# Gate chain, decays, key and value rows and output gating moved under the input projection; linear-attention outputs with tokens on partitions

## The chip, the cores and the metric

The kernel runs on one core of one Trainium2 chip. Its time is the time on the device of one execution, in microseconds; the median of three runs is shown. A profile was taken of one further execution.

## What is computed

One inference step of a one-layer hybrid decoder: 1024 prompt tokens and 8 new tokens (each with 4096 past tokens), width 1024, all in fp32. Cut to what matters here:

```python
h = rms_norm(x, norm_mix_pre)
z = h @ w_in       # gq 256, gk 256, gv 512, gr 512, glr 16, nq 512, nkv 768, ng 24 columns
g = log_sigmoid(glr @ w_gla_gate + b_gla_gate) / 16
# gated linear attention, 4 heads, chunks of 64 tokens:
b  = cumsum(g, within the chunk)
qe = gq * 64 ** -0.5 * exp(b)
a  = tril(qe @ (gk * exp(-b)).T)
o  = a @ gv + qe @ S
S  = exp(b_last) * S + (gk * exp(b_last - b)).T @ gv
y_gla = rms_norm(o, per head) * gain * silu(gr)
# native sparse attention, 8 query heads, 2 key heads: compressed keys and values
# (a convolution of 32 rows with stride 16, + pe, gelu, @ w2), selected blocks, a window,
# mixed by sigmoid(ng); with 1024 tokens the prompt selects every block
x += rms_norm(concat(y_gla, y_nsa) @ w_out)
x += rms_norm(relu(rms_norm(x) @ w_ff_up) ** 2 @ w_ff_down)
```

The new tokens take one step of the recurrence each, with their own state, and attend to their paged cache. Outputs are also the new key and value rows, the window rows and the states.

## The kernel before

Phases follow each other, each a block with one instruction stream per engine; a phase starts when all engines have left the one before: load, norm, input projection, middle phase, prompt attention, sample attention, output projection, norm, feed-forward, norm. Activations lie features on partitions: `hT` is the normed input (8 tiles of 128 features by 1032 tokens), `Z` holds the projected tiles (24 of them).

**Dense phases.** Input projection, output projection and feed-forward use Strassen's way of multiplying with seven products (helper `seven_products`, matmul at L291). A pair of output tiles is seven products M1, M2, M6, M5, M7, M3, M4 in that order, each of 16 matmuls (32 instructions for two, since an fp32 matmul is two instructions of which the profile counts each). The products accumulate in PSUM banks and are evicted by ScalarE (M1, M6, M5, M4: L526 in the projection) or added by VectorE (M2, M7, M3: L546). GpSimd makes four sums of weight blocks per pair (`weight_sums`, L254 to L261). The banks are given by `bank_of`: M1, M6, M7 and M4 use banks 0 and 1 or 2 and 3 by turns from pair to pair, M2 banks 4 and 5, M5 and M3 banks 6 and 7. M1 waits for the eviction of M4 two pairs back, M2 for that of M2 one pair back, M6 for M1, M7 for M6, M3 for M5, M4 for M7 of the same pair. The weights of a pair lie in one of two slots of `ring`; SP asks for pair n once M4 of pair n - 2 is done. The projection has 11 such pairs, the output projection 4, the feed-forward 32. In half of the feed-forward's pairs (down, all but the first group) VectorE evicts all seven.

**Small products.** After the 11 pairs the projection multiplies the 40 columns of the gates (16 of rank, 24 of the sigmoid gates) with all tokens (L517), in three parts of 344 tokens, and ScalarE evicts them.

**Middle phase** (`phase_mid`), in the order of TensorE: the gate products (L863, 16 rows deep); the transposes of key and value rows of each 128 tokens (`kv_rows`, L760 and L763, two row buffers in `srow`, evicted by ScalarE and VectorE by turns and stored by SP), with outer products for the new tokens' states between them (L771, from diagonals that GpSimd makes, L696); then the recurrence in eight steps of 128 tokens: scores (L796), state increments (L809), transposes of the next values and keys (L782, L784, evicted by ScalarE, L938 and L939), outputs (L821 within the chunk, L828 with the state); then the new tokens' outputs (L893, one column each), the bias products of the compression (L848, one column each), the compression's convolutions (L857) and the squares for the norm of the outputs (L839, ones times squares), and two last small products. Beside it ScalarE makes softplus, the exponentials of the decays, the sigmoids of `gr` and the root of the norm (as exponential of a logarithm, L1009 and L1014), VectorE the running sums (L1036), the decayed queries and keys (L1049 to L1053), mask (L1061), states (L1075) and at the end the gating (L1190, L1192). The outputs have features on partitions. ScalarE's queue asks for a 4 MB copy of the window rows from one DRAM tensor to another at the start (L957).

**Attention** (`phase_attend`) first scales the queries on VectorE (L1384) and its scores (L1415) wait for that.

What follows attention is touched by the change in one place only, the banks of the dense phases.

Of the kernel before, what the change touches and what calls it, by code (L numbers as in the profile page):

```python
# [80 lines left out]
def layout(nc, ctx, M):  # L81
# [29 lines left out]
    M.PS = ctx.enter_context(nc.psum_tensor("PS", [P, 8, 512], FP32))  # L111
    M.sems = {}
# [124 lines left out]
def bank_of(M, n, e):  # L237
    return {M1: 2 * (n % 2), M6: 2 * (n % 2), M7: 2 * (n % 2), M4: 2 * (n % 2), M2: 4, M5: 6, M3: 6}[e]
# [25 lines left out]
def seven_products(nc, M, pe, st, n, data, before):  # L264
# [37 lines left out]
def phase_norms(nc, M, A, O, use, front, back):  # L302
# [20 lines left out]
    with nc.Block() as block:  # L323
        @block.sync
        def _(sp):
            if use == 0:
                for s in range(2):
                    sp.dma_start(pair_slot(M, s), A["w_in"][0, :, 2 * s * P:2 * (s + 1) * P]
                                 .rearrange("(k p) c -> p k c", p=P)).then_inc(M.sem(f"pair{s}_loaded"), 16)
            elif back is not None:  # L330
# [130 lines left out]
def phase_project(nc, M, A):  # L461

    NP = 11
    w_in = A["w_in"][0].rearrange("(k p) c -> p k c", p=P)
    hsum, small_l, small = M.sem("proj_summed"), M.sem("small_loaded"), M.sem("small_done")
    Xf = M.X[:, :, :].rearrange("p a n -> p (a n)")
    h11, h12, h21, h22 = (M.hT[:, h * KQ:(h + 1) * KQ, t * HN:(t + 1) * HN] for h in range(2) for t in range(2))
    t1, t2, t3 = (Xf[:, i * KQ * HN:(i + 1) * KQ * HN].rearrange("p (k n) -> p k n", n=HN) for i in range(3))
    t4 = M.srow[:, 0:KQ * HN].rearrange("p (k n) -> p k n", n=HN)
    wsm = M.Zf[:, 23 * N:23 * N + KD * (RANK + NGATE)].rearrange("p (k c) -> p k c", k=KD)  # L470
    parts = [1] * 6 + [4] * 2 + [1] * 3
    st = M.dense = Seven(M, ["first"] * NP, parts, M.srow[:, 2064:3600], M.dense)

    def tiles(n):
        return M.Z[:, 2 * n, :], M.Z[:, 2 * n + 1, :]

    with nc.Block() as block_:
        @block_.sync
        def _(sp):
            for n in range(2, NP):  # L480
                st.wait_product(sp, n - 2, M4)
                w = pair_slot(M, n)
                if n < 6 or n >= 8:
                    c = 2 * n * P if n < 6 else C_KV + 2 * (n - 8) * P
# [87 lines left out]
def phase_mid(nc, M, A, O):  # L572
# [53 lines left out]
    def by(t):  # L626

        return rows[t % 2], t // 2 + 1
# [1586 lines left out]
```

## Time and profile before

| | |
|---|---|
| median of 3 runs | 2159.88 us (2159.83 to 2160.62) |
| the profiled execution's own time | 2160.74 us |
| its span in the profile | 2159.0 us |
| mean granted TensorE clock | 0.95 |
| TensorE busy | 1951.8 us, 90% of the span |
| ScalarE / VectorE / GpSimd busy | 492.3 / 699.1 / 618.0 us |

The profile gives, for each instruction, engine, line of the kernel, tiles and duration, and for idle time of an engine what ended it. PE is TensorE, PEld its weight loads, DVE VectorE, ACT ScalarE, POOL GpSimd, SP the engine that issues most transfers.
### The profile page before, as it was taken

Reading aid. Unit: us, or ns where it says so; the run is one execution under the profiler, and the core shown is the slowest. Engines: PE = TensorE matmul, PEld = TensorE weight load, DVE = VectorE, ACT = ScalarE, POOL = GpSimd, SP = SyncE. Lnnn points to the kernel's source line nnn. Section 1 sums busy time; section 2 is a strip of 40 time slices with the busy share of each in tenths; the row PEclk is TensorE's granted clock in tenths of the full one; section 3 lists DMA queues with packets and bytes.
Section 4 is the critical chain, followed back from the end, with each engine's and each line's share of the span. In section 5 each row is a group of like instructions: output and inputs, shape, how many; then the busy total and the mean of one; then the engine's idle time right before and its main releaser. Section 6 shows DMA issues by size and latency. Waiting matters only on the chain. (4 is left out here: it accounts for less than half of the span.)

```text
span 2159.0 us, 25959 instructions
## 1 busy us (share of the span) xinstructions
PE 1951.8 (90%) x10618; PEld 1554.0 (72%) x10618; DVE 699.1 (32%) x1541; ACT 492.3 (23%) x1089; POOL 618.0 (29%) x526
## 2 busy tenths in 40 slices
PE   3999995785899968999997996999999999999997
PEld 3888882572444436777775886888888888888885
DVE  2300002627565533423332107530132223213313
ACT  2001102334555543434332014101010000001002
POOL 0411212104888762111110304312221122111223
PEclk9999996787999988999998997999999999999998
DMA  4112104101000017665650411111111111111111
GB/s 119 38 45 39 40 20 147 41 23 40 1 1 1 1 34 262 226 200 189 224 178 30 133 36 25 38 40 39 40 40 59 39 40 39 46 52 39 40 50 79
DMA packets 121806, 149.62 MB, mean 69 GB/s; under 512 B 29888, under 2 KB 107496, under 8 KB 113432
## 3 DMA queue, kind: packets, MB, share of 16 engines
q1 hardware_dynamic: 109824, 76.64, 12.2%
q0 software_dynamic: 9216, 67.11, 9.3%
q10 hardware_dynamic: 2648, 4.21, 0.5%
q8 instruction: 84, 1.38, 0.3%
q14 instruction: 34, 0.28, 0.0%
HBM read 139.86 MB, written 12.27 MB: 70 GB/s over the span
## 5 line engine op out<-in xcount | busy, mean ns | idle before, releaser
L291 PE MATMUL PS<-Z,ring 128*128 128x258 f32 x1152 | 258.2, 380 | 0.0
L1581 PE MATMUL PS<-Z 128*128 128x256 f32 (+1 forms) x1024 | 244.6, 385 | 0.0
L291 PEld LDWEIGHTS PS<-Z,ring 128*128 128x128 f32 x1152 | 218.2, 189 | 32.9
L291 PE MATMUL PS<-hT,ring 128*128 128x258 f32 x992 | 224.9, 384 | 8.8 <-DMA ring<-in_w_out 7.7
L254 POOL TENSOR_TENSOR Z<-ring 128x512 f32<-128x512 f32 x36 | 48.7, 1353 | 602.1 <-PE PS L291 532.7
L291 PEld LDWEIGHTS PS<-hT,ring 128*128 128x128 f32 x992 | 190.0, 192 | 38.2 <-DMA ring<-in_w_out 7.7
L1581 PEld LDWEIGHTS PS<-Z 128*128 128x128 f32 x1024 | 186.5, 190 | 43.0 <-issue 20.5
L2127 ACT ACTIVATE Z<-PS 128x516 f32<-128x516 f32 x80 | 48.0, 600 | 646.8 <-PE PS L291 646.8
L291 PE MATMUL PS<-Z 128*128 128x258 f32 x832 | 187.1, 380 | 0.0
L291 PEld LDWEIGHTS PS<-Z 128*128 128x128 f32 x832 | 157.5, 189 | 23.9
L2147 DVE TENSOR_TENSOR Z<-PS,Z 128x516 f32<-128x516 f32 x96 | 66.8, 696 | 314.9 <-PE PS L291 314.9
L291 PE MATMUL PS<-hT,Z 128*128 128x258 f32 x640 | 145.9, 380 | 0.0
L1544 POOL DMA_INDIRECT Z<-in_cache_nsa_kv,idx x64 | 60.2, 941 | 275.1 <-ACT X L1766 101.9
L291 PEld LDWEIGHTS PS<-hT,Z 128*128 128x128 f32 x640 | 121.1, 189 | 18.4
L1285 POOL TENSOR_SCALAR Z<-Z,misc 128x63 f32<-128x63 f32 (+7 forms) x87 | 99.4, 1161 | 85.2 <-DVE misc L1370 85.0
L1872 DVE STREAM_TRANSPOSE Z<-Z 128x1024 f32<-128x1024 f32 x64 | 79.1, 1239 | 128.2 <-DMA Z<-in_cache_nsa_kv,idx 116.5
L2153 DVE TENSOR_TENSOR Z<-PS,Z 128x516 f32<-128x516 f32 x48 | 33.4, 695 | 254.6 <-PE PS L291 254.6
L1415 PE MATMUL PS<-Z 64*128 64x512 f32 (+3 forms) x384 | 85.7, 525 | 19.8 <-DVE Z L1384 17.4
L291 PE MATMUL PS<-srow,ring 128*128 128x258 f32 x432 | 98.5, 380 | 0.0
L546 DVE TENSOR_TENSOR Z<-PS,Z 128x516 f32<-128x516 f32 x33 | 22.9, 695 | 231.0 <-PE PS L291 231.0
L291 PEld LDWEIGHTS PS<-srow,ring 128*128 128x128 f32 x432 | 81.8, 189 | 12.3
L363 PE MATMUL PS<-Z,X 128*128 128x128 f32 x256 | 40.8, 332 | 51.5 <-DVE Z L440 39.1
(352 smaller groups left out, 2860.3 us busy)
## 6 DMA issues: line engine op xcount, KB each, us to landing
ring<-in_w_ff_up SPq DMA_DIRECT2D x32, 512.0 KB, 5.5
ring<-in_w_ff_down SPq DMA_DIRECT2D x32, 512.0 KB, 4.4
ring<-in_w_in SPq DMA_DIRECT2D x9, 1024.0 KB, 5.2
X<-in_x_prompt SPq DMA_DIRECT2D x8, 1024.0 KB, 11.3
srow<-in_state_nsa_win SPq DMA_DIRECT2D x16, 256.0 KB, 5.8
out_y_prompt<-X SPq DMA_DIRECT2D x8, 512.0 KB
out_win_sample<-in_state_nsa_win ACTq DMA_DIRECT2D x1, 4088.0 KB
ring<-in_w_in SPq DMA_DIRECT2D x8, 256.0 KB, 4.4
```

Source lines behind the costliest of these rows:

```text
L254: pool.tensor_tensor(st.s1, block(w, 1, 0), block(w, 1, 1), ALU.add).then_inc(st.sums_r, 1)
L291: last = nc.tensor.matmul(M.PS[:, bank_of(M, n, e) + c, 0:CW], a[:, k, :], b[:, k, c * CW:(c + 1) * CW], start=e in (M1, M2, M5) and k == ...
L363: last = nc.tensor.matmul(M.PS[:, 4 + 2 * s + k // 4, (k % 4) * P:(k % 4) * P + n], x_tile(M, t)[:, k * P:(k + 1) * P], diag[0:n, s, 0:n], ...
L546: nc.vector.tensor_tensor(halves(out), bank_view(M, n, e), halves(out), ALU.add).then_inc(st.dve, 1)
L1285: last = pool.tensor_scalar(p_of(n, g, kvh)[:, c:c + w], p_of(n, g, kvh)[:, c:c + w], rc[:, m % NSLOT, br, kvh:kvh + 1], None, ALU.mult)
L1415: last = nc.tensor.matmul(M.PS[:, 2 * (cc % 2) + kvh, at:at + w], M.Z[r, Z_Q + 2 * gp + g, qt * P:(qt + 1) * P], k, start=True, stop=True)
L1544: pool.indirect_dma_start(Zf[:, 4096 + n % NS * 2048:4096 + (n % NS + 1) * 2048], None, cache, bass.IndirectOffsetOnAxis(M.idx[:, n:n + 1] ...
L1581: last = nc.tensor.matmul(out, w1s[:, v, half, 2 * r + e, :], x2[seg][:, r, v, :, e, half:half + SEG[seg]], start=(j == 0), stop=(j == 15))
L1872: nc.vector.transpose(x2b[seg][:, :, :, c:c + 32], raw[:, n % NS, :, 0:2, :].rearrange("p r w (k x) -> p r (w k) x", x=32)).then_inc(xt, 1)
L2127: nc.scalar.activation(halves(place(*tiles(n), e)), bank_view(M, n, e), ACT.Relu if e == M4 and kinds[n] == "up" else ACT.Copy).then_inc(s ...
L2147: nc.vector.tensor_tensor(halves(out), bank_view(M, n, e), halves(out), ALU.add).then_inc(st.dve, 1)
L2153: nc.vector.tensor_tensor(halves(out), bank_view(M, n, e), halves(out), ALU.add).then_inc(st.dve, 1)
```

## The change

The order of the pairs in the projection becomes 0, 1, 8, 9, 10, 4, 5, 2, 3, 6, 7 (queries and keys of the linear attention, the sparse attention's keys and values, `gr`, `gv`, the sparse attention's queries). M2 moves from banks 4 and 5 to the pair of banks that M4 of the previous pair used, in all dense phases, so that banks 4 and 5 are free. In a slot numbered 7 n + e stands product e of pair n, and the work of the old middle phase is put at given slots of each engine's stream: the small products before pair 0, gate products before M2 and M6 of pair 0, softplus, running sums, decays, decayed queries and keys in pairs 0 to 2, constants in pairs 2 to 4, the row transposes before slots 36, 39, ... 60, the sigmoids and the gating of `gr` in pairs 6 and 7. The last two pairs (queries) are evicted with a scale. SP stores rows between weight loads and asks for state and convolution weights at the end of the projection.

In the middle phase the outputs of a step have tokens on partitions (the operands of the two output products are swapped); ScalarE squares them, VectorE sums, ScalarE takes the root, VectorE its reciprocal, GpSimd makes four diagonal tiles, and a matmul with these turns the scaled outputs back to features on partitions; VectorE multiplies them with the gated `gr`. The new tokens' states come from products of masked keys, one token in each step. The bias columns of the compression ride in its convolutions. GpSimd and VectorE share the rearrangement of the compression's rows. The copy of the window rows moves to SP at the start of attention, and attention's query scaling is gone.

```diff
 def bank_of(M, n, e):
-    return {M1: 2 * (n % 2), M6: 2 * (n % 2), M7: 2 * (n % 2), M4: 2 * (n % 2), M2: 4, M5: 6, M3: 6}[e]
+    return {M1: 2 * (n % 2), M6: 2 * (n % 2), M7: 2 * (n % 2), M4: 2 * (n % 2), M2: 2 - 2 * (n % 2),
+            M5: 6, M3: 6}[e]
...
-        if e == M1 and n >= 2:
-            st.wait_moved(pe, n - 2, M4)
+        if e == M1 and n >= 1:
+            st.wait_moved(pe, n - 1, M2)
         if e == M2 and n >= 1:
-            st.wait_moved(pe, n - 1, M2)
+            st.wait_moved(pe, n - 1, M4)
...
+            small_products()
+            for n in range(NP):
+                def before(e):
+                    if n == 0 and e in (M6, M5, M7, M4):
+                        pe.wait_ge(hsum, {M6: 2, M5: 2, M7: 3, M4: 4}[e])
+                    if n == 0 and e in (M2, M6):
+                        gate_products(0 if e == M2 else 1)
+                    if n == 0 and e == M5:
+                        pe.wait_ge(gmv, 2)
+                    for t in range(QT + 1):
+                        if 7 * n + e == turn_at(t):
+                            kv_rows(t)
```

ScalarE's stream in the projection:

```diff
+            for n in range(NP):
+                for e in range(7):
+                    slot = 7 * n + e
...
+                    if slot in (1, 2):
+                        gate_move(slot - 1)
+                    if slot == 4:
+                        soft_plus(0)
+                        soft_plus(1)
+                    if slot == 5:
+                        act.wait_ge(soft_r, 2)
+                        soft_log(0)
+                        soft_log(1)
+                    if slot == 11:
+                        decays()
+                    if slot == 15:
+                        late_decays()
```

TensorE's stream in the middle phase:

```diff
+            def outputs(t):
...
+                        nc.tensor.matmul(M.PS[:, OB + q, a * P:(a + 1) * P], Am[:, t % 2, q, a, :],
+                                         vtk[:, t % 2, 2 * a + q, :], start=(a == 0), stop=False, skip_group_check=True)
...
+                            last = nc.tensor.matmul(M.PS[c * CHUNK:(c + 1) * CHUNK, OB + q, a * P:(a + 1) * P],
+                                                    M.Z[r, Z_GQ + a, t * P + c * CHUNK:t * P + (c + 1) * CHUNK],
+                                                    Sr[r, (2 * t + c) % 5, a, :],
+                                                    start=False, stop=True, skip_group_check=True)
+                last.then_inc(orr, 1)
+
+            def turn_back(t):
+                pe.wait_ge(dgr, t + 1)
+                pe.wait_ge(amr, min(t + 3, QT))
+                if t >= 1:
+                    pe.wait_ge(fin, t)
+                for j in range(GH):
+                    last = nc.tensor.matmul(M.PS[:, X + j // 2, 256 + j % 2 * P:256 + (j % 2 + 1) * P], Osb[:, t % 2, j, :], dg[:, t % 2, j, :],
+                                            start=True, stop=True)
+                last.then_inc(ybk, 1)
...
             for t in range(QT):
+                if t >= 2:
+                    turn_back(t - 2)
                 if t + 1 < QT:
                     scores(t + 1)
                     increments(t + 1)
                 if t + 2 < QT:
                     turn(t + 2)
                 outputs(t)
+            turn_back(QT - 2)
+            new_outputs()
+            compress(0)
...
+            turn_back(QT - 1)
+            compress(1)
```

ScalarE's stream in the middle phase:

```diff
             def vk(t):
-                act.wait_ge(vtd, t + 1)
+                act.wait_ge(vtd, t + 2)
                 if t >= 2:
                     act.wait_ge(orr, t - 1)
...
+            def scale(t):
+                act.wait_ge(ssr, t + 1)
+                nc.scalar.activation(root[:, t, :], ssum[:, t, :], ACT.Sqrt, bias=M.eps[:, 0:1], scale=1.0 / DV)\
+                  .then_inc(rtr, 1)
...
             for t in range(QT):
                 if t + 2 < QT:
                     vk(t + 2)
+                if t >= 1:
+                    scale(t - 1)
                 out(t)
```

Attention, VectorE and then TensorE:

```diff
-            for g in range(G):
-                nc.vector.tensor_scalar(M.Z[:, Z_Q + g, 0:T], M.Z[:, Z_Q + g, 0:T], M.qsc[:, g:g + 1], None,
-                                        ALU.mult).then_inc(q_r, 1)
...
-            pe.wait_ge(q_r, G)
```

## Rows read from the trace of the kernel before

**Rows 1.** Table by stage: start:end, length, then busy us, PEclk, DMA share, GB/s.

```profile
79.70:323.92 244.22, 244.22 (x1121) 211.93 (x1120) 20.87 (x30) 24.01 (x40) 45.29 (x36) 1.00 0.15 40
...
339.40:390.90 51.50, 25.32 (x86) 13.32 (x86) 17.64 (x38) 16.37 (x25) 18.86 (x23) 0.55 0.51 165
...
408.00:444.20 36.20, 28.99 (x388) 25.02 (x380) 27.62 (x65) 15.05 (x33) 0.66 (x1) 0.99 0.12 35
444.20:463.00 18.80, 18.66 (x128) 18.56 (x128) 4.41 (x13) 4.27 (x7) 3.90 (x7) 0.56 0.00 0
463.00:496.50 33.50, 16.85 (x96) 13.92 (x96) 9.83 (x8) 13.22 (x16) 0.00 (x0) 0.81 0.00 1
```

**Rows 2.** Timeline, TensorE: small products, gate products, attention's first scores.

```profile
323.92 14.07 PE L517 MATMUL PS<-hT,Z 128*40 128x344 f32 x48
...
339.41 5.95 PE L863 MATMUL PS<-Z,wg 16*128 16x344 f32 x12 [1.41 <-PEq L477]
...
500.50 2.08 PE L1415 MATMUL PS<-Z 64*128 64x256 f32 x8 [17.44 <-DVE Z L1384]
```

**Rows 3.** Waits from 320 to 530 us: who waited for whom.

```profile
DVE Z L1190 <- ACT Z L1014: 37.2, 1, 37.2
...
PE PS L1415 <- DVE Z L1384: 17.4, 1, 17.4
PE PS L760 <- ACT srow L925: 16.6, 2, 16.2
```

**Rows 4.** Timeline: one step of the recurrence, TensorE and ScalarE's first copy.

```profile
417.72 0.66 PE L782 MATMUL PS<-ident,Z 128*128 128x128 f32 x4
...
418.43 1.06 PE L821 MATMUL PS<-srow,X 128*128 128x128 f32 x8
...
419.42 1.11 PE L828 MATMUL PS<-Z,srow 64*128 64x64 f32 x16
...
420.36 0.67 PE L796 MATMUL PS<-Z,X 64*128 64x128 f32 x8
420.63 0.60 ACT L938 ACTIVATE X<-PS 128x512 f32<-128x512 f32 x1 [3.03 <-PE PS L828]
...
421.56 0.69 PE L809 MATMUL PS<-X 64*64 64x128 f32 x16 [0.53 <-ACT X L939]
...
422.18 0.66 PE L782 MATMUL PS<-ident,Z 128*128 128x128 f32 x4
```

**Rows 5.** Groups by line, 320 to 530 us: busy us, mean ns of one.

```profile
L760 PE MATMUL PS<-ident,Z 128*128 128x128 f32 x48 | 12.3, 429 | 22.1 <-ACT srow L925 16.6 <-DVE srow L1032 4.6 <-ACT X L965 1.0
...
L696 POOL TENSOR_TENSOR Z<-ident,zs 128x512 f32<-128x512 f32 x8 | 9.0, 1131 | 30.1 <-PE PS L771 30.1
```

**Rows 6.** Timeline: two products, an eviction, ScalarE's table load and two exponentials.

```profile
128.52 7.14 PE L291 MATMUL PS<-hT,ring 128*128 128x258 f32 x32
...
132.21 0.60 ACT L526 ACTIVATE Z<-PS 128x516 f32<-128x516 f32 x1 [2.89 <-PE PS L291]
...
347.92 1.28 ACT L969 ACT_TABLE_LOAD   x1
...
349.22 2.02 ACT L969 ACTIVATE X<-X 128x1032 f32<-128x1032 f32 x2
```

**Rows 7.** Timeline of the first norm: one root and one reciprocal.

```profile
34.32 0.29 ACT L396 ACTIVATE Z<-Z,eps 128x1 f32<-128x1 f32 x1
...
34.64 0.16 DVE L418 RECIPROCAL Z<-Z 128x1 f32<-128x1 f32 x1 [34.64 <-ACT Z L396]
```

**Rows 8.** Timeline, TensorE: new tokens' outputs, and one convolution.

```profile
444.21 4.92 PE L893 MATMUL PS<-misc,hT 64*128 64x1 f32 x64 [0.76 <-ACT hT L945]
...
472.14 3.73 PE L857 MATMUL PS<-hT,ring 128*128 128x126 f32 x32
```

**Rows 9.** Transfers by line: KB of one piece, us to landing.

```profile
hT<-in_state_gla SPq DMA_DIRECT2D x1, 0.5 KB, 25.8
```

**Rows 10.** Table by stage, 4 us late in the recurrence.

```profile
436.00:440.00 4.00, 2.56 (x40) 2.09 (x38) 3.24 (x8) 3.07 (x6) 0.00 (x0) 1.00 0.63 195
```

More of the change, by code:

```diff
@@ L888, in _ @@
-            pe.wait_ge(oev, QT)
-            for b in range(B):
-                for a in range(2):
-                    for q in range(2):
-                        r = slice(q * DK, (q + 1) * DK)
-                        last = nc.tensor.matmul(M.PS[:, OB + q, a * B + b:a * B + b + 1], state[r, b, a, :],
-                                                qs[r, a, b:b + 1], start=True, stop=True)
-            last.then_inc(so, 1)
-            compress_bias()
-            compress(0)
-            squares(0)
@@ L910, in _ @@
[L910 to L912 removed]
+            small_products()
[10 more added lines that the diff above has]
+                            kv_rows(t)
+                seven_products(nc, M, pe, st_, n, (h11, h21, h22, t1, t2, t3, t4), before)
@@ new lines, in soft_plus, with soft_log, decays @@
+            def soft_plus(a):
+                act.wait_ge(neg, a + 1)
+                nc.scalar.activation(soft[a], soft[a], EXP).then_inc(soft_r, 1)
+            def soft_log(a):
+                act.wait_ge(soft_r, a + 1)
+                nc.scalar.activation(soft[a], soft[a], ACT.Ln, bias=M.one[:, 0:1]).then_inc(soft_r, 1)
+            def decays():
+                act.wait_ge(scan, 4)
+                for a in range(2):
+                    g = gate_pair(M, a)[:, :, 0:HT2]
+                    nc.scalar.activation(up[a].rearrange("p (h n) -> p h n", h=2), g, EXP, scale=1 / 16)
+                    nc.scalar.activation(M.ends[:, a, :].rearrange("p (h c) -> p h c", h=2), g[:, :, CHUNK - 1:HT2:CHUNK],
+                                         EXP, scale=1 / 16)
+                    nc.scalar.activation(down[a].rearrange("p (h n) -> p h n", h=2), g, EXP, scale=-1 / 16).then_inc(exr, 1)
+                act.wait_ge(g_ready, 2)
+                nc.scalar.activation(M.eg.rearrange("p (h i) a -> p a h i", h=2),
+                                     M.hT[:, 0:4, HN + HT2:N].rearrange("p (a h) i -> p a h i", h=2), EXP, scale=1 / 16)
@@ L968, in _ @@
-            for a in range(2):
-                nc.scalar.activation(soft[a], soft[a], EXP, scale=-1.0).then_inc(soft_r, 1)
-            act.wait_ge(soft_r, 2)
-            for a in range(2):
-                nc.scalar.activation(soft[a], soft[a], ACT.Ln, bias=M.one[:, 0:1]).then_inc(soft_r, 1)
-            kv_rows(0)
-            kv_rows(1)
-            act.wait_ge(g_ready, 2)
-            nc.scalar.activation(eg.rearrange("p b a -> p a b"), G[:, :, T:N], EXP, scale=1 / 16).then_inc(egr, 1)
-            kv_rows(2)
@@ L978, in _ @@
-            decays(0)
-            for t in range(3, QT + 1):
-                kv_rows(t)
-            act.wait_ge(sgl, 48)
-            nc.scalar.activation(M.sg[:, :, :], M.sg[:, :, :], EXP, scale=-1.0).then_inc(sgate, 1)
-            decays(1)
-            vk(0)
-            vk(1)
-            for t in range(QT):
-                if t + 2 < QT:
-                    vk(t + 2)
-                if t >= 4:
-                    sigmoid(t - 4)
-                out(t)
-            act.wait_ge(so, 1)
```

1177 lines of the change are left out of this document (648 added, 529 removed).

## The prediction

> **What bounds the kernel now.** The chain that ended last covers only the final norm, so I read a table by stage first, then the waits and the timeline around the stage that changes. From 79.70 to 323.92 the projection keeps TensorE busy all the time at granted clock 1.00, while ScalarE works 24.01 us and VectorE 20.87 us of 244.22 [rows 1]. Its last dense product ends at 323.92; then 14.07 us of small products, and the middle phase from 339.4; attention's first matmul starts at 500.50 [rows 2]. In those 176.58 us TensorE is mostly not the limit: 25.32 us busy of 51.50 at clock 0.55 while the gates and the rows are made, 28.99 of 36.20 at 0.99 in the recurrence, 16.85 of 33.50 at the end [rows 1]. The waits say why: transposes wait 16.6 us for a row buffer, VectorE waits 37.2 us for the exponentials of the output norm, and attention's first score waits 17.4 us for VectorE (the last gating and the query scaling) [rows 3]. Work of ScalarE and VectorE lies beside an idle TensorE here, and beside a full one in the projection. So the question is what the projection can cover, and what is left.
>
> **What moves under the projection.** TensorE's own part is not hidden, it is added. Small products: the same 1032 columns in 64 instructions in place of 48, 14.1 us [rows 2], now first. Gate products: 5.95 us at the half clock [rows 2], so 3.0 at the full one, with eight short instructions more; bounds 3.0 and 5.95, taken 3.7. Row transposes: 54, and 8 of the small tile, 62 in all. Four took 0.66 us in the recurrence, 0.165 each with the switch [rows 4], and 48 took 12.3 us, 0.256 each, at the half clock [rows 5]: 10.2 to 15.9; below, 0.11 each without a switch would give 6.8. I take 10, since the clock is full there. The dense products then end at 323.92 + 14.1 + 3.7 + 10 = 351.7.
>
> The rest I cost at nothing, and the cover is this. A pair has seven products of 3.49 us (32 instructions of two products took 7.14 us, the last one's drain included [rows 6]). An eviction is due one product after its own product ends and takes 0.60 us, so anything up to 2.9 us may stand ahead of one that is due, and ScalarE's free slot between M5 and M4 is 10.5 us long. The largest packets: exponential and logarithm, two table loads of 1.28 us and four passes of 1.0 to 1.1 us (two took 2.02) [rows 6], 6.8 us from the end of M5 of pair 0, ready 3.7 us before M4 is; the decays, 6.1 us in the same place of pair 1; VectorE's chunk ends and queries, about 6 us after M3, where its next duty is M2 of the next pair, 10 us on. The small gate weights are two loads more on SP during the first norm, 20 us before use. On SP the small convolution constants go out 40 us before the first load of the projection is released, and row stores ahead of the load for two pairs on, while that load's own release (M4 two pairs back) is still to come, and weight sums have five products of slack for the two copies of kept values on GpSimd. M2 now takes the bank pair that M4 of the previous pair has just left: it waits for that eviction, ready 0.60 us into an M1 of 3.49 us, here and in all later dense phases. Nothing stalls. Without that cover the packets would cost their length, some 6 us each.
>
> Gone with no new place: the query scaling before attention (folded into the last evictions), the 64 one-column bias products (now columns inside the convolutions), the 24 squares products, the logarithms and exponentials of the output norm, and the copy of the window rows as a neighbour of the row loads (4 MB, it moves to SP's queue at the head of attention, whose compute reads nothing from DMA; it costs nothing there, and if it held up the sample weights queued behind it, the sample phase would start late, not attention).
>
> **What is left in the middle phase.** It starts 1.4 us after the last product (338.0 to 339.4 [rows 2]), at 353.1; the last eviction and SP's request for the last convolution weights lie in that gap. Prices of one step of the recurrence come from one period of before [rows 4]: six transposes 0.71 (417.72 to 418.43), eight 128-wide products 0.99 (to 419.42), sixteen narrow products 0.94 (to 420.36), eight scores about 0.55 (0.67 with their drain), sixteen increments 0.61 (421.56 to the next transposes). After: the cross products are sixteen 64x64 tiles like the increments, 0.61; the turn back costs another 0.99; the new tokens' outer products eight instructions, between 0.45 and 0.85, taken 0.45. Sum 0.71 + 0.99 + 0.61 + 0.55 + 0.61 + 0.99 + 0.45 = 4.9 us against 3.8 of work in a period of 4.46 before.
>
> But TensorE will not reach 4.9. The turn back of tile u stands at the head of step u + 2, right behind the outputs of u + 1. It needs the diagonals of u (GpSimd), these the reciprocal (VectorE), this the root (ScalarE), and the root stands in ScalarE's queue behind the value and key copies of tile u + 3, which wait for the outputs of u + 1, the very product that TensorE has just ended. So each turn back pays in series: copies 0.93 (from the start of the first at 420.63 to the increments that wait for both at 421.56 [rows 4]), root 0.29, reciprocal 0.16 [rows 7], diagonals 1.13 [rows 5], five hand-overs of some 0.05: 2.6 us of idle TensorE. Period 2.6 + 4.9 = 7.5 us. VectorE is not the limit: mask, mix, states, new state, inverse and sums are about 4.2 us.
>
> Steps: prologue and steps 0 and 1 about 17 us (two rounds of copies, masked keys and first states, 15 us at full clock, 2 more for a start at the half one); step 2 with the first root's table load 1.28, 8.9; steps 3 to 5 three times 7.5; step 6 without a transpose 6.8; step 7, whose root is free early, 4.2. Sum 59.4. Tail: turn back 1.4, one-column outputs 4.92 [rows 8], two convolutions with 189 columns in place of 126, each 3.73 x 1.5 = 5.6 bounded below by 5.0, taken 5.0 for weight loads already in the 3.73, turn back 0.9, activation 0.7, last products 0.7, copies 0.5: 19.1, and 2 for the half clock that followed the one-column products of before (0.56 from 444.20 on [rows 1]). Middle phase 80.5 us. The state rows are asked for after the last M5, three products or 10.5 us before the end, and are due some 7 us into the phase. They took 25.8 us before, beside the 4 MB copy [rows 9]; without it I expect well under the 17.5 us that are covered, and at the old price they would cost 8 us.
>
> Attention starts at 353.1 + 80.5 + 0.4 = 434.0 instead of 500.50: 66.5 us gained. The profiled execution took 2160.74 us (span 2159.0), 0.86 above the median shown; 2160.74 - 66.5 = 2094.2, on the median's scale 2093.
>
> **Two rules weighed.** The step above mixes 64-row, 64x64 and full tiles. Before, sixteen 64x64 products took 0.69 us with their drain, a quarter of their serial length, and the changes of shape between groups are inside the 4.46 us period [rows 4]. The Trainium skill, "TensorEngine Tiling (Array Packing)", Key Properties, says that changing the tiling mode drains the engine. By that rule the two or three further changes of shape per step would each add about a drain, 0.2 us by four transposes' 0.66 less four times 0.12, some 4 us over the phase, 2097; I leave it in the range. And TensorE idles 2.6 us in 7.5: before, it was busy 2.56 of 4.00 us at clock 1.00 [rows 10]. The Trainium skill, "TensorE: Matmul & The Clock Gate", HAM oscillation, says that waits between bursts can throttle the engine again and again; that is the second rival.
>
> **Rivals.**
> First, the serial hand-over is hidden: TensorE is work-bound at 4.9 us a step. For it: before, steps were nearly work-bound. Against: the queue order. It saves about 5 x 2.6 + 1.3: 2079. Chance 0.12.
> Second, the clock stays at 1.2 GHz through the recurrence. Price: work at the half clock is 8.6 where it is 4.9, 3.7 us in six steps, and 5 in the tail: 27, giving 2120. For it: 0.55 and 0.56 in the light stretches of before [rows 1]. Against: the row of 4.00 us above, and 0.99 in the old recurrence. Chance 0.17.
> Third, the packets do delay evictions, or the row transposes cost the half-clock price: 6 to 30 us over eleven pairs, 2099 to 2123. Chance 0.12.
> Fourth, slower: M2's new wait binds in all 47 pairs (11, 4 and 32). It decides once the eviction of M4 comes more than 3.49 us after its product; to eat 66.5 us it must be late by 1.4 us in each, so 4.9 us after, eight times its 0.60 us; late by 1.6 us the kernel takes 2093 + 47 x 1.6 = 2168. The place where VectorE evicts M4 itself is the down pairs, where it queues only behind adds of its own pair, one per product. Chance 0.03.
> Fifth, the change doesn't do what it says: the state at its old price, the stores late, and step 0 waits for them, 8 to 20 us, 2101 to 2113. Chance 0.02.
>
> **Numbers.** Forecast 2093, chance 0.54. Faster by over 0.2% (4.3 us, about what a measurement of this kernel tells from no change) in all cases but the fourth, less 0.02 that sums of them end near no change: 0.95; same 0.02; slower 0.03. Range: below to the first rival less 3 (bound of the transposes), 2076; above to the second with a microsecond more, 2121. Outside lie the fourth, the dearest part of the third and the sums of second and third.
>
> **What would show it.** Right: dense products end near 352 with no gap above 0.3 us beside the inserted groups; the turn back in the trace waits about 2.6 us for GpSimd in steps 2 to 6, released by its diagonals; step period 7.5 us; attention at 434; everything behind it as long as before (1660.2 us). Wrong: waits of M4 or M6 for ScalarE or VectorE in the projection; a clock of 0.50 in the steps; a dense pair in the later phases above 24.4 us; a first score that waits for anything but the phase's end.

## The result, and the profile after

The changed kernel takes 2111.24 us (median of 4 runs, 2108.29 to 2112.09) against 2160.25 (4 runs of the kernel before), a ratio of 0.9755 with the interval [0.9737, 0.9774]. Forecast were 2093 and a range of 2076 to 2121: the sign and the range held, the forecast was 18 us too low. The profiled execution took 2112.03 us.

The page of the changed kernel, total and the granted clock in 40 slices:

```profile
span 2110.3 us, 26095 instructions
...
PEclk9999999779999979999997998999999999999998
```

The table by stage of the changed kernel (start:end, length, then busy us of PE, PEld, DVE, ACT and POOL, clock, DMA share, GB/s). It answers to [rows 1]:

```profile
54.90:351.60 296.70, 296.69 (x1382) 250.98 (x1382) 69.78 (x106) 54.26 (x86) 72.16 (x82) 1.00 0.18 49
353.10:372.20 19.10, 17.31 (x174) 13.30 (x174) 8.02 (x25) 4.64 (x11) 9.43 (x10) 0.73 0.18 56
372.10:430.80 58.70, 44.21 (x380) 36.38 (x376) 24.80 (x66) 14.07 (x30) 11.09 (x14) 0.68 0.06 18
400.00:404.00 4.00, 4.00 (x35) 3.34 (x32) 2.86 (x9) 0.00 (x0) 0.00 (x0) 0.50 0.00 0
404.00:408.00 4.00, 1.52 (x21) 1.05 (x19) 0.28 (x2) 2.17 (x5) 0.99 (x2) 0.89 0.01 2
420.00:424.00 4.00, 4.00 (x38) 3.21 (x36) 1.35 (x3) 0.00 (x0) 0.00 (x0) 0.50 0.00 0
430.80:453.00 22.20, 20.25 (x157) 19.71 (x155) 3.84 (x12) 4.79 (x14) 1.58 (x2) 0.85 0.04 10
```

First row: the projection, small products included, is one block of TensorE work with no gap, at clock 1.00, and carries 69.78 us of VectorE, 54.26 of ScalarE and 72.16 of GpSimd. It ends at 351.6, where 351.7 was forecast. The inserted products in the timeline of TensorE (the first and the last line are cut off by the ends of the stretch that was asked for; the small products take 14.11 us in all):

```profile
54.91 3.44 PE L687 MATMUL PS<-hT,Z 128*40 128x258 f32 x15 [0.58 <-PEq L326]
...
72.64 2.33 PE L701 MATMUL PS<-Z,wg 16*128 16x258 f32 x12
...
211.03 0.82 PE L713 MATMUL PS<-ident,Z 128*128 128x128 f32 x6
211.78 0.25 PE L716 MATMUL PS<-ident,Z 40*128 40x40 f32 x1
211.96 2.23 PE L294 MATMUL PS<-X,ring 128*128 128x258 f32 x9
```

None has an idle time in front beyond the 0.58 us at the stage's start. The gate products took twice 2.33 us and a tile's rows 0.93 (211.03 to 211.96). Every product stands in an unbroken queue, so the bank pair that M2 now shares costs nothing.

All of the miss is in rows two and three. From 353.1 to 430.8 the recurrence takes 77.7 us, forecast 59.4. One step of it, in the timeline of TensorE:

```profile
393.95 0.67 PE L1166 MATMUL PS<-hT,Z 64*64 64x128 f32 x16
397.19 1.29 PE L1178 MATMUL PS<-Z 128*128 128x128 f32 x8 [2.57 <-POOL Z L1060]
398.41 1.23 PE L1127 MATMUL PS<-Z 64*128 64x128 f32 x8
399.57 0.69 PE L1139 MATMUL PS<-misc,hT 8*64 8x128 f32 x4
...
400.61 1.13 PE L1145 MATMUL PS<-srow 64*64 64x128 f32 x16
401.67 1.11 PE L1114 MATMUL PS<-ident,Z 128*128 128x128 f32 x4
...
403.00 1.91 PE L1157 MATMUL PS<-srow,X 128*128 128x128 f32 x8
404.85 0.67 PE L1166 MATMUL PS<-hT,Z 64*64 64x128 f32 x16
```

The step is 10.9 us long (393.95 to 404.85), not 7.5. Its wait is as forecast: 2.57 us ahead of the turn back (L1178), ended by GpSimd's diagonals (L1060). Its work is not: the first product behind the wait is nearly at full pace (1.29; 1.16 at its best), then four transposes take 1.11 us where they took 0.66 [rows 4] and eight output products 1.91 where they took 1.06. That is the half clock, which the windows 400 to 404 and 420 to 424 show as 0.50 with TensorE busy all the time. After it the clock is back (L1166 0.67), and the next wait follows. In the other four steps of this kind the turn back itself runs slowly, in 1.90 to 2.08 us: the clock has fallen by the time the wait ends. The wait itself, link by link (ScalarE, VectorE and GpSimd in the timeline, behind the outputs of 404.85):

```profile
405.66 0.60 ACT L1250 ACTIVATE srow<-PS 128x512 f32<-128x512 f32 x1 [8.70 <-PE PS L1166]
406.15 0.38 ACT L1251 ACTIVATE srow<-PS 128x256 f32<-128x256 f32 x1
406.42 0.30 ACT L1267 ACTIVATE X<-X,eps 128x4 f32<-128x4 f32 x1
...
406.75 0.18 DVE L1343 RECIPROCAL X<-X 128x4 f32<-128x4 f32 x1 [3.04 <-ACT X L1267]
...
407.01 1.04 POOL L1060 TENSOR_TENSOR Z<-ident,X 128x512 f32<-128x512 f32 x1 [9.25 <-DVE X L1343]
```

It is the chain of the forecast in the forecast's order: copies, root, reciprocal, diagonals. Over the phase it makes

```profile
PE PS L1178 <- POOL Z L1060: 15.1, 7, 4.1
```

which is 15.1 us in seven waits. Attention's first score comes at 453.00 (forecast 434.0), waits for nothing but the phase's end, and what follows takes 1657.3 us (1658.5 before: 2159.0 - 500.5).

So TensorE idles as long as I said, and works longer than I said because its clock falls. Two theories for that stood against each other: the waits lower the clock (A), or the narrow and mixed shapes of the step do (B).

### The profile page after: what moved, and what is told of

Read it like the earlier page. It is cut to its first block and busy times, and to the rows that moved or that the text cites. A ratio compares the mean times of both kernels' runs of the same rounds, so it can differ in the third digit from the quotient of the medians.

```text
span 2110.3 us, 26095 instructions
## 1 busy us (share of the span) xinstructions
PE 1944.7 (92%) x10662; PEld 1555.4 (74%) x10662; DVE 695.5 (33%) x1550; ACT 488.9 (23%) x1091; POOL 618.6 (29%) x534
## 5 line engine op out<-in xcount | busy, mean ns | idle before, releaser
L2342 DVE TENSOR_TENSOR Z<-PS,Z 128x516 f32<-128x516 f32 x96 | 66.8, 696 | 314.8 <-PE PS L294 314.8
L2348 DVE TENSOR_TENSOR Z<-PS,Z 128x516 f32<-128x516 f32 x48 | 33.4, 696 | 254.6 <-PE PS L294 254.6
L1487 POOL TENSOR_SCALAR X<-X,misc 128x63 f32<-128x63 f32 (+5 forms) x60 | 75.5, 1280 | 18.2 <-DVE misc L1572 18.2
```

The costliest lines, as they stand in the source:

```text
L1487: last = pool.tensor_scalar(p_of(n, g, kvh)[:, c:c + w], p_of(n, g, kvh)[:, c:c + w], rc[:, m % NSLOT, br, kvh:kvh + 1], None, ALU.mult)
L2342: nc.vector.tensor_tensor(halves(out), bank_view(M, n, e), halves(out), ALU.add).then_inc(st.dve, 1)
L2348: nc.vector.tensor_tensor(halves(out), bank_view(M, n, e), halves(out), ALU.add).then_inc(st.dve, 1)
```

## The experiments

Ratios are to the kernel before, run beside each on the same chip. Its own median was 2160.25 us beside the changed kernel, 2168.67 beside the first three experiments and 2161.0 to 2163.4 beside the others, so ratios of different groups can be compared only to about 0.004. All else comes from the profiled executions, one for each kernel.

### The root ahead of the copies

```
-                if t + 2 < QT:
-                    vk(t + 2)
                 if t >= 1:
                     scale(t - 1)
+                if t + 2 < QT:
+                    vk(t + 2)
                 out(t)
```

> Changed kernel, with one edit on ScalarE: in each step of the recurrence the root of tile t - 1 stands ahead of the value and key copies of tile t + 2. Measured before this run: 2.57 us of idle TensorE ahead of each turn back, steps of 10.9 us, granted clock 0.68 over the steps. Theory A (the serial hand-over idles TensorE, and the idle time is what lowers the clock): the wait shrinks to what VectorE's order leaves, under 1 us, the clock goes to 1.00 in the steps, a step takes 5 to 6 us, the kernel 2080 to 2088 us. Rival B (the clock is low because of the shapes, 64x64 and 8-row products, whatever the idle time): only the waits go, steps of about 8.3 us, 2097 to 2100 us. Rival C (another wait takes its place at once, the value copies now being later): steps stay near 10.9 us, 2108 us or more.

Measured: 0.9636 [0.962, 0.9652]. The waits of the turn back fall from 15.1 to 10.1 us, a saving of 5, but the span falls by 17.1 us, 2110.3 to 2093.2. Steps take 6.2 to 7.0 us once the clock is back. Table by stage, then the waits:

```profile
353.10:366.40 13.30, 11.99 (x100) 9.20 (x101) 5.45 (x18) 2.64 (x7) 9.24 (x10) 0.64 0.28 79
...
372.00:410.90 38.90, 29.96 (x376) 24.66 (x376) 23.81 (x66) 12.97 (x28) 10.61 (x14) 0.96 0.08 23
```
```profile
PE PS L1178 <- POOL Z L1060: 10.1, 7, 2.1
```

The shapes are the same as in the changed kernel, and the clock is 0.96 in place of 0.68. This favours A. The waits that are left in steps 3 to 7, of 0.9 to 1.7 us each, did not bring the clock down: it is 1.00 from 381.7 to 410.9.

### The inverse to the head of VectorE's step as well

```
             for t in range(QT):
+                if t >= 1:
+                    inverse(t - 1)
                 if t + 1 < QT:
                     mask(t + 1)
...
-                if t >= 1:
-                    inverse(t - 1)
                 sums(t)
```

> As e1, and on VectorE the reciprocal of tile t - 1 moves from behind the states of step t + 1 to the head of the step. Theory A: the rest of the wait goes too, 0.5 to 0.9 us in each of five or six steps, so 2 to 5 us below e1, near 2079 us. Rival: the reciprocal was not what the diagonals waited for, and the time is that of e1 within 1 us. Under rival B both are near 2097 us.

Measured: 0.9613 [0.9596, 0.963], span 2081.5. The wait is gone from the steps; 2.0 us in two waits are left, and TensorE is busy 27.70 of 27.90 us:

```profile
372.10:400.00 27.90, 27.70 (x374) 22.88 (x372) 22.78 (x63) 11.96 (x26) 9.60 (x12) 1.00 0.01 2
...
400.10:424.60 24.50, 21.86 (x154) 21.31 (x155) 4.52 (x14) 4.78 (x14) 2.08 (x2) 0.79 0.17 49
```

A step is now 5.2 us of work from one L1166 to the next (386.73 to 391.95). By starts in its timeline:

```profile
386.73 0.67 PE L1166 MATMUL PS<-hT,Z 64*64 64x128 f32 x16
387.33 1.16 PE L1178 MATMUL PS<-Z 128*128 128x128 f32 x8
388.42 0.72 PE L1127 MATMUL PS<-Z 64*128 64x128 f32 x8
389.06 0.43 PE L1139 MATMUL PS<-misc,hT 8*64 8x128 f32 x4
...
389.65 0.67 PE L1145 MATMUL PS<-srow 64*64 64x128 f32 x16
390.25 0.66 PE L1114 MATMUL PS<-ident,Z 128*128 128x128 f32 x4
```

Turn back 1.09, scores 0.64, new tokens' products 0.59, where I had 0.99, 0.55 and 0.45; the rest is as priced. Those three are the 0.3 us a step by which my 4.9 was short. The tail grew from 22.2 to 24.5 us, its clock 0.79: the next thing to look at.

### The wait filled with unread products

```
                 outputs(t)
+                if 1 <= t <= 5:
+                    pe.wait_ge(str_, 2 * (t + 2))
+                    warm(9 if t == 1 else 6)
```

Here `warm` issues products of 128 x 256 into a free part of bank 1 that nobody reads; the rest is the changed kernel.

> Changed kernel, with work added: behind the outputs of steps 1 to 5 TensorE multiplies six (step 1: nine) 128x256 blocks whose product nobody reads, into a free half of bank 1, about 2.6 us at the full clock, as long as the wait for the turn back. All waits stay. Theory A (idle time lowers the clock): the clock stays at 1.00 from the first filled step on, a step takes 7.5 us as the prediction had it, and the kernel with more work gets faster, 2093 to 2098 us. Rival B (the shapes lower the clock): each filling takes 5.2 us at the half clock where 2.6 us were idle, so the kernel gets slower, 2120 us or more. Half way: the clock goes up in some steps, 2100 to 2110 us.

Measured: 0.9672 [0.9656, 0.9688], span 2096.9. Work was added, none taken away, and the kernel is 13.4 us shorter than the changed one by the spans (12.7 by the medians; 0.0083, or 18 us, by the ratios, which come from different groups). The six-fold filler takes 2.69 us (389.15 to 391.84) where the wait was 2.57:

```profile
372.10:416.40 44.30, 42.63 (x442) 35.46 (x442) 24.36 (x66) 14.08 (x30) 10.56 (x13) 1.00 0.07 20
```
```profile
389.15 2.86 PE L1210 MATMUL PS<-Z 128*128 128x256 f32 x12
391.84 1.11 PE L1178 MATMUL PS<-Z 128*128 128x128 f32 x8
```

The same narrow products run at 1.00 once TensorE does not stand still between them. The filler is wide, so this run by itself could also mean that wide products lift the clock; the run before it had none of them, no wait in the steps either, and 1.00 as well. For the recurrence A is shown by the two together, and B falls. A step is 7.85 us, 5.2 of work and 2.6 of filled wait, what the forecast had meant by 7.5. This also splits the prize of the version before: against the changed kernel, 13.4 us are clock. Against this one the kernel with root and inverse first is another 15.4 us shorter (2096.9 - 2081.5); the missing waits are 15.3 of it (steps 2 to 7 take 29.1 us in place of 44.4), and what else differs cancels: a full clock in its first steps (3.8 us) against a later start of the phase (2.7) and a longer tail (1.8).

### The banks alone, on the kernel before

```
-    ... M2: 4, M5: 6, M3: 6}[e]
+    ... M2: 2 - 2 * (n % 2), M5: 6, M3: 6}[e]
...
-        if e == M1 and n >= 2:
-            st.wait_moved(pe, n - 2, M4)
-        if e == M2 and n >= 1:
-            st.wait_moved(pe, n - 1, M2)
+        if e == M1 and n >= 1:
+            st.wait_moved(pe, n - 1, M2)
+        if e == M2 and n >= 1:
+            st.wait_moved(pe, n - 1, M4)
```

> Kernel before, with the new banks and waits of M2 alone, in all 47 pairs. My theory: the eviction of M4 ends 0.6 us into an M1 of 3.49 us, so nothing waits: 2158 to 2162 us, a pair of 24.4 us. Rival (M2's new wait binds): every late microsecond of the eviction counts 47 times, 2170 us or more.

Measured: 0.9991 [0.9978, 1.0003], span 2158.8. TensorE's only wait in dense products is the one for `w_out` that the kernel before has too:

```profile
PE PS L291 <- DMA ring<-in_w_out: 7.7, 1, 7.7
```

The spare banks cost nothing that can be measured in 47 pairs. The fourth rival falls.

### The 4 MB copy moved, on the kernel before

```
-            act.dma_start(O["win_sample"][0, :, 0:WIN - 1]..., A["state_nsa_win"][0, :, 1:WIN]...)
+            sp.dma_start(O["win_sample"][0, :, 0:WIN - 1]..., A["state_nsa_win"][0, :, 1:WIN]...)
```

The second line stands at the head of SP's stream in attention.

> Kernel before, with the 4 MB copy of window rows moved from the head of the middle phase to SP at the head of attention, and nothing else. Theory: part of the gain was only that this copy no longer stands in the way of state, row stores and convolution weights (the state took 25.8 us to land, ScalarE waited 15.5 us for a row store): 12 to 20 us faster, 2140 to 2148 us. Rival (the stage was bound by its own chains, the transfers only seemed to be waited for): under 4 us, 2156 us or more. If the copy disturbs attention, its time grows beyond 1658.5 us from its first score to the end.

Measured: 0.9957 [0.9941, 0.9973], span 2154.9 (2159.0). By the transfers of this kernel

```profile
hT<-in_state_gla SPq DMA_DIRECT2D x1, 0.5 KB, 6.8
```

the state lands in 6.8 us, which took 25.8 [rows 9]: the copy had been what slowed it. The wait of 16.2 us for a row buffer [rows 3] became one of 8.5, now for VectorE's eviction, and attention's first score came 4.1 us earlier (496.43). I had expected 12 to 20: when the copy goes, the next wait of the same chain takes over. So of the 47.5 us that attention's start gained, these two traces give the copy 4. The ratio over all executions gives it more, 9 us with an interval of 6 to 13; the profiled execution was one of the slower of ten (2156.64; 2148.6 to 2160.48), and where the rest of the 9 us lies is not shown.

### More work on ScalarE in pair 1

```
+                    for i in range(6):
+                        if a or i:
+                            act.wait_ge(S("cover"), 6 * a + i)
+                        nc.scalar.activation(down[a]..., g, EXP, scale=-1 / 16).then_inc(S("cover"), 1)
+                    act.wait_ge(S("cover"), 6 * a + 6)
                     nc.scalar.activation(down[a]..., g, EXP, scale=-1 / 16).then_inc(exr, 1)
```

> The changed kernel with twelve extra exponential passes of about 1.1 us on ScalarE in pair 1 of the projection, chained behind the decays (13 to 14 us more in its free slot). Theory of the prediction (a packet is free until it is more than one further product late, since M2 of the next pair waits for M4's eviction): the slot has 4.3 us idle and M1's product of 3.5 us to spare, so TensorE waits once, 6 to 7 us, ahead of M2 of pair 2, and every later event is 6 to 7 us later; ratio to the changed kernel 1.003. Rival (the moved steps cost something even where no wait is seen, for instance through slower evictions): waits in several places and more than 9 us in all, or the packet costs its full 13 us. Other rival: it is hidden altogether, no wait.

Measured: 0.98 [0.9778, 0.9822], 0.0045 above the changed kernel; medians 2118.28 and 2111.24, spans 2114.3 and 2110.3. ScalarE's two blocks of six passes took 6.49 and 6.48 us, so 13 us of work were added, and in the whole projection TensorE waited once:

```profile
PE PS L294 <- ACT Z L836: 5.8, 1, 5.8
```

This takes the rule by which I had costed 54 us of ScalarE work at nothing past its limit: of 13 us the slot and the product behind it swallowed 7.2, near the 7.8 that the rule gives, and the rest was waited for. One size of load was tried. The wait cost more than its own length: the product behind it took 5.31 us (132.39) where its neighbours take 3.65, with a granted clock of 0.50 up to 135 us, and the middle phase began 7.8 us later (360.86, 353.10 in the changed kernel), 5.8 of wait and 1.9 of clock. The first score comes only 4.05 us later (457.05), because the phase's first steps drew a better clock in this execution: from its start to the first L1166 product it took 10.0 us where the changed kernel, with the same code there, took 13.3. From there to the first score both take the same (86.2 and 86.6 us).

### Both convolutions ahead of the one-column products

Root and inverse first, and in the tail:

```
             turn_back(QT - 2)
-            new_outputs()
             compress(0)
-            pe.wait_ge(soe, 2)
-            ...
-            turn_back(QT - 1)
             compress(1)
+            turn_back(QT - 1)
+            new_outputs()
+            pe.wait_ge(soe, 2)
+            ...
```

ScalarE's tail follows: last root, both activations, then the new tokens.

> The kernel with the root and the inverse put first, and in its tail both convolutions and the last turn back now stand ahead of the 64 one-column products. Theory (the one-column products, though back to back, lower the clock for what follows them): the convolutions take about 5.3 us each at full clock instead of 7.9 and 5.3, the one-column products 4 to 6 us behind them, and root, inverse and gating of the new tokens follow; the tail shrinks from 24.5 us to 19 to 21 us and attention's first score comes at 419 to 421 instead of 424.6; ratio to before 0.959 to 0.9605. Rival (the clock falls in the tail by the convolution's own narrow products or by time since the recurrence): the first convolution takes 7.9 us again in the new place, the tail stays at 23 to 25 us.

Measured: 0.9633 [0.9617, 0.9648], span 2081.8: nothing gained. The timeline shows both halves of it:

```profile
399.21 10.41 PE L1205 MATMUL PS<-X,ring 128*128 128x189 f32 x64
409.45 1.05 PE L1178 MATMUL PS<-Z 128*128 128x128 f32 x8
410.44 3.74 PE L1190 MATMUL PS<-misc,X 64*128 64x1 f32 x64
...
418.04 2.08 PE L1612 MATMUL PS<-Z 64*128 64x256 f32 x8 [1.84 <-PEq L1038]
```

The convolutions take 5.2 us each, as expected, and attention starts 6.6 us sooner (418.04, 424.61 before). But its first eight products take 2.08 us where they took 1.14, and from there to the end it is 1663.8 us where it was 1656.9. Attention as a whole, to its last product, takes 307.9 us where it took 300.0; its first 17 us have a granted clock of 0.50 in place of 0.78, the next 83 us 0.88 in place of 0.96, with TensorE as busy as before in these 83. The half clock was not removed, it was pushed behind the phase's end, and what the tail had won was given back there.

### A one-column product after each convolution product

```
                 for j in range(16):
                     last = nc.tensor.matmul(M.PS[:, CONV[v], 0:3 * NCP], ...)
+                    if j < 15:
+                        column(16 * v + j)
```

> The kernel with both convolutions ahead, and now one one-column product after each of the 32 convolution products, instead of 32 one-column products in a row. Theory (a stretch in which TensorE does nothing but one-column products lowers the clock of what follows; it was paid in the convolutions before, and in attention's first products when the convolutions stood ahead): with wide products between them the clock stays at 1.00 through the tail and into attention; convolutions and columns together 13 to 15 us, attention's first score near 418, its first eight products 1.14 us again instead of 2.08, and the remainder from there 1657 us instead of 1664; whole span near 2075, ratio to before 0.957 to 0.959. Rival (attention's slow start is the wait at the phase's boundary, not the columns): first eight products 2.08 us again, span 2080 to 2082.

Measured: 0.9748 [0.9735, 0.9762], span 2111.9, 30 us longer than its neighbour, and the worst miss of the study. TensorE shows no gap, and stands at 0.50 from 403 to 447 us:

```profile
412.00:424.00 12.00, 12.00 (x35) 8.21 (x34) 0.00 (x0) 0.09 (x1) 0.00 (x0) 0.50 0.00 0
...
434.00:444.00 10.00, 10.00 (x28) 6.91 (x28) 0.00 (x0) 0.00 (x0) 0.00 (x0) 0.50 0.01 2
```
```profile
405.56 1.00 PE L1203 MATMUL PS<-X,ring 128*128 128x189 f32 x2
406.48 0.58 PE L1190 MATMUL PS<-misc,X 64*128 64x1 f32 x2
407.00 1.00 PE L1203 MATMUL PS<-X,ring 128*128 128x189 f32 x2
```

A pair is 1.44 us. Either the changes between 128-row and 64-row products do this, or the columns do.

### Columns in blocks; and as many changes without columns

The first issues eight columns after every eighth convolution product (four blocks). The second keeps the columns in a row behind the convolutions, and puts between convolution products an unread product of 64 rows and 128 columns:

```
+                    if j < 15:
+                        nc.tensor.matmul(M.PS[:, 1, 256:256 + P], M.Z[0:DK, Z_GR, 0:P],
+                                         M.Z[0:DK, Z_GR + 1, 0:P], start=True, stop=True)
```

> As the kernel with a one-column product after each convolution product, but in blocks: eight convolution products, then eight one-column products, four times. The alternation ran at 0.50 for 45 us though TensorE showed no gap, 0.93 us per convolution product where the same product takes 0.66 us at half clock in a row of its own. Theory A (each change between 128-row and 64-row products drains the array, and the drains, not the columns, took the clock): seven changes instead of 63, clock 0.90 to 1.00 in the tail, attention's first score at 416 to 420, span 2075 to 2080. Theory B (the one-column work itself takes it, wherever it stands): the clock falls behind the first block of columns, the convolutions behind it take 0.66 us each, attention at 423 to 428, span 2083 to 2090.

> The kernel with both convolutions ahead (columns in one row behind them), and after each convolution product but the last an unread product of 64 rows and 128 columns, so that the array changes between 128 and 64 rows as often as with the columns between. Theory A (the changes drain the array and take the clock): clock 0.50 again in the convolutions, over 1.4 us per pair of products, some 45 us for the tail. Theory B (the one-column products take it): clock 1.00, a pair costs 0.33 us plus 0.12 to 0.25 us, so the convolutions take 15 to 19 us instead of 10.4.

Measured, blocks: 0.9643 [0.9629, 0.9656], span 2079.6. Measured, half rows between (one execution): 2099.24 us, span 2097.5. Two rows of the first kernel's table by stage, then one cycle of the second:

```profile
399.28:414.16 14.88, 14.88 (x131) 13.94 (x129) 1.81 (x7) 2.40 (x6) 1.04 (x1) 1.00 0.13 36
418.09:424.00 5.91, 5.79 (x28) 4.08 (x28) 3.56 (x23) 3.42 (x10) 0.00 (x0) 0.50 0.65 221
```
```profile
406.31 0.59 PE L1205 MATMUL PS<-X,ring 128*128 128x189 f32 x2
406.82 0.49 PE L1208 MATMUL PS<-Z 64*128 64x128 f32 x2
407.24 0.59 PE L1205 MATMUL PS<-X,ring 128*128 128x189 f32 x2
```

The same 32 columns in blocks of eight: clock 1.00. The same number of changes with wide columns: clock 1.00 too (400 to 432), but a cycle of 0.93 us where the two products in rows of their own take 0.33 and 0.16. So two changes cost 0.44 us, 0.22 each, when every product is a change; both convolutions took 28.6 us (401.75 to 430.37), where 15 to 19 were expected. Neither as many changes with 128-column products nor the columns in blocks of eight take the clock; one column after each product did, and both theories were half right. Columns in one row of 32 are a third case: in the changed kernel and the first three experiments the first convolution stands right behind them and takes 7.1 to 8.4 us, the second 5.3. With blocks, attention's first products are again at half clock (2.08 us from 418.09), behind a gap of 2.15 us.

### Nothing narrow last

Eight columns after every fourth product of the first convolution, then the last turn back, the new tokens' sum, and the second convolution unbroken; the new tokens' root is taken under it.

> Root and inverse first, and the tail ordered so that nothing narrow stands last: four products of the first convolution, eight one-column products, four times; last turn back; the sum over the new tokens' squares; the second convolution, wide and unbroken, under which ScalarE and VectorE finish the new tokens. Theory (the time won in the tail so far was given back as half clock in attention's first products, because columns and a 2.2 us gap stood right ahead of them; columns in blocks between wide products leave the clock at 1.00): clock 1.00 from 371 to the end of the phase, attention's first score at 417 to 418.5, its first eight products 1.14 us and not 2.08, 1657 us from there to the end; span 2073.5 to 2076, ratio to before 0.957 to 0.960. Rival (what comes early is given back in attention whatever stands ahead of it, since its pace is set elsewhere): first eight products 1.14 us, but still 1661 us or more from there, span 2079 to 2081.

Measured: 0.9624 [0.961, 0.9637]. Its profiled execution, at 2085.48 us the slowest of five (the others 2079.88 to 2081.62), lost the clock in the fourth block (eight convolution instructions 2.89 us at 408.94, 1.55 before), so the first score came at 424.65, and its first eight products took 1.13 us. Inconclusive: the theory's 2073 to 2076 did not come. The four versions with root and inverse first lie at 0.9613, 0.9633, 0.9643 and 0.9624 with intervals of 0.0013 to 0.0017 to each side. No tail is shown to beat the simplest of them, the one that moves only root and inverse, and which of the four is the fastest is not settled: by the medians the order is 2084.99, 2083.55, 2083.03 and 2081.45, but the first was measured beside the slowest group of the kernel before. The simplest lies below the changed kernel by 28.8 us by the spans, 26 by the medians and 0.0142 (31 us) by the ratios.

## Why the prediction was right or wrong

- **Projection as cover: right.** Dense products end at 351.6, forecast 351.7. Terms: small products 14.1 (14.11 measured), gate products 3.7 (4.66), row transposes 10 (0.93 for each of eight tiles and 0.7 for the small one, 8.1). The terms sum to 26.9 against 27.8; the 0.8 between that and the matching end I have not traced. The cover's limit was tested: 7.2 us of 13 swallowed, where 4.3 of idle time and M1's 3.5 make 7.8; that a wait behind it costs clock as well (1.9 us) was not in the rule.
- **The new waits of M2: right at nothing**, by the banks alone.
- **The serial hand-over: right**, 2.57 us a step for 2.6, with each link in its place; the first rival (hidden) falls. That it fits to 0.03 us is luck: the links as I priced them (0.93, 0.29, 0.16, 1.13 and five hand-overs of 0.05) add up to 2.76, not to the 2.6 that I wrote. The two reorderings remove it, one instruction each.
- **The work of a step, 4.9 us: 0.3 short**, 2 us over the phase, in the three groups that stand next to a change of shape. The Trainium skill, "TensorEngine Tiling (Array Packing)", Key Properties, had been weighed for that: a change of tiling mode drains the engine. The trace agrees in kind: 0.22 us a change where every product is one, about 0.1 in the step; I had left it out of the sum, and my estimate of 4 us for it would have been 2 too dear.
- **The clock: the step that failed.** I put the second rival at 0.17 and the clock of the step at full, on a 4 us window at 1.00 in which TensorE was busy 2.56 us [rows 10]. That window was the wrong witness: it shows the clock of a moment, not what a 2.6 us stop in every step does to the step behind it. Measured from 372.1 to 430.8: 0.68. With the wait filled, the steps end at 416.4 and not at 430.8, so 14.4 of the 18.3 us that the recurrence was late are clock. Of the other 3.9, 1.9 are my prices of the steps and 2.0 the start, which is clock too: 19.0 us where I had 17, of it 2 for the half clock, and 15.3 where it ran at the full one (root and inverse first). The Trainium skill, "TensorE: Matmul & The Clock Gate", HAM oscillation, describes the same pattern, waits between bursts that throttle the engine again and again, for a kernel whose waits are 3 to 5 us long; the trace agrees with waits of 2.6 us, 0.50 with TensorE full in 400 to 404 and 0.89 in the next 4 us. The second rival's price of 27 us supposed the half clock throughout; the mean of 0.68 lies between the two levels, and so does the loss. I had treated as two cases what was a mixture. The range held because its upper end came from this rival, not because the forecast's own mechanism covered it.
- **Tail: 22.2 for 21.5** with the hand-over to attention, state rows not waited for, attention and all behind it as long as before. The third and fifth rivals fall with the rows above; the state rows landed in 6.2 us.

In sum: nothing at the projection's end, +18.3 in the recurrence, +0.7 in the tail, -1.2 behind it: the 17.8 us by which the profiled execution (2112.03) lies above its forecast of 2094.2.

Open: why the first 13 us of the middle phase ran at 0.65 in the changed kernel and at 1.00 with root and inverse first. The edit is not needed for it: with more work on ScalarE in pair 1 the middle phase has the changed kernel's code and ran there at 1.00 as well. And where attention's start stands with a tail that holds the clock in every execution: none here did.

## What to carry to other kernels

Price a wait of TensorE twice: its own length, and the products behind it at half clock. Here waits of 2.6 us, in steps that take 7.8 us with the wait filled, cost another 1.5 to 3.3 each, and a single one of 5.8 us in the projection cost another 1.9; waits of 0.9 to 1.7 us, once in each step, cost only themselves (clock 1.00). Where the wait can't be removed, look first at whether one small instruction (a root, a reciprocal) stands in its engine's queue behind bulk copies that wait for the very product just issued; failing that, unread products in the gap paid for themselves. And follow a gain past the stage's end before you count it: 6.6 us won in the tail were gone again within attention.

## What was not expected of the hardware

- Adding 33 unread products of 256 columns made the kernel 13 us faster by the trace.
- TensorE can be fully busy for 44 us and stay at 0.50: one-column products of 64 rows alternating with products of 128 rows and 189 columns. In blocks of eight the same products run at 1.00.
- The clock's level at a given place differs between executions of the same code: the middle phase's first steps, to the first L1166 product, took 13.3 us in the changed kernel and 10.0 with the extra passes in pair 1, which leave this phase's code alone. A single trace places such a stretch only to within some microseconds.
- The state's transfer of 0.5 KB pieces takes 6.8 us without a 4 MB copy beside it and 25.8 with one.
